# GpSimd's six low parts of weight chunks given to VectorE, and the orders of three engines written anew

## The reference

```
x = x + mla_mixer(rms_norm(x)); x = x + sq_relu_mlp(rms_norm(x))
x = x + moba_mixer(rms_norm(x)); x = x + sq_relu_mlp(rms_norm(x))
h = x + rms_norm_2(gdn_mixer(rms_norm_2(x)))
k, v, c = shared_kv(h)
out = h + rms_norm_2(fox_mixer(rms_norm_2(h), k, v, c))
```

## Time and profile before

| | |
|---|---|
| median of 3 runs | 920.63 us (919.89 to 922.73) |
| the profiled execution's own time | 920.44 us |
| its span, first to last instruction | 918.7 us |
| busy: TensorE, VectorE, ScalarE, GpSimd | 97%, 68%, 57%, 9% |
| mean granted TensorE clock | 0.991 |

### The profile page before, as it was taken

How to read it: one execution, slowest core, us unless ns; L and a number is a source line. 1 busy time by engine, 2 the same in 40 slices (tenths; PEclk the granted TensorE clock), 3 DMA queues, 4 the chain that set the end, 5 groups by cost and what they waited for, 6 DMA issues and landing times.

```text
span 918.7 us, 13095 instructions
## 1 busy us (share of the span) xinstructions
PE 892.3 (97%) x5254; PEld 775.3 (84%) x5254; DVE 623.6 (68%) x1033; ACT 525.6 (57%) x848; POOL 78.4 (9%) x96
## 2 busy tenths in 40 slices
PE   6899999999999999999999999999999999999997
PEld 6877888888888888888888888999988887798885
DVE  6887676766666576657655556696786666776775
ACT  5888544435444686636444434566546565657782
POOL 0055000000000000000000000002536312000000
PEclk9999999999999999999999999999999799999999
DMA  7451456535654544446555654554430041654411
GB/s 261 139 164 67 138 183 247 186 138 184 210 195 145 183 139 146 151 153 238 181 187 182 222 191 138 187 165 157 138 106 32 9 153 46 207 189 180 167 64 46
DMA packets 61677, 142.67 MB, mean 155 GB/s; under 512 B 5296, under 2 KB 7344, under 8 KB 61616
## 3 DMA queue, kind: packets, MB, share of 16 engines
q1 hardware_dynamic: 61616, 141.83, 45.0%
HBM read 140.77 MB, written 1.05 MB: 154 GB/s over the span
## 4 chain that ended last, share of the span: by engine, by line
PE 90%; DVE 3%; POOL 3%; issue 2%; ACT 1%; DMA 1%; SPq 0%; DVEq 0%; ACTq 0%; POOLq 0%
PE ps L491 86%; PE ps L499 4%; POOL arena L3531 3%; DMA X<-x_dram 1%; ACT whi L1382 1%; DVE sub L2315 1%; ACT arena L1382 1%; DVE wlo L2315 0%; DVE xhl L2315 0%; POOL otl L3531 0%; DVE X L2315 0%; DVE arena L2321 0%; DVE arena L2315 0%; ACT otl L1382 0%; DVE X L2321 0%
## 5 line engine op out<-in xcount | busy, mean ns | idle before, releaser
L2315 DVE TENSOR_TENSOR wlo<-raw,whi 128x2048 fp32r<-128x2048 f32 (+3 forms) x130 | 286.8, 2215 | 121.7 <-ACT whi L1382 121.4
L1382 ACT ACTIVATE whi<-raw 128x2048 fp32r<-128x2048 f32 (+3 forms) x136 | 250.7, 1851 | 179.0 <-PE ps L491 164.1
L491 PE MATMUL ps<-xhl,whi 128*128 128x512 f32 (+3 forms) x928 | 216.4, 345 | 0.0
L491 PE MATMUL ps<-whi,xhl 128*128 128x512 f32 (+2 forms) x528 | 168.7, 387 | 1.2 <-DVE xhl L2321 1.0
L491 PE MATMUL ps<-whi,oth 128*128 128x512 f32 x416 | 164.6, 396 | 0.2 <-DVE otl L2321 0.2
L491 PEld LDWEIGHTS ps<-xhl,whi 128*128 128x128 f32 (+2 forms) x928 | 150.8, 187 | 14.4 <-DVE xhl L2321 0.8
L491 PE MATMUL ps<-whi,otl 128*128 128x512 f32 x416 | 162.4, 390 | 0.0
L491 PE MATMUL ps<-wlo,oth 128*128 128x512 f32 x416 | 162.2, 390 | 0.0
L491 PE MATMUL ps<-xhl,wlo 128*128 128x256 f32 x720 | 140.1, 281 | 0.0
L491 PEld LDWEIGHTS ps<-xhl,wlo 128*128 128x128 f32 x720 | 116.8, 187 | 11.2
L491 PEld LDWEIGHTS ps<-whi,xhl 128*128 128x128 f32 x528 | 99.4, 190 | 18.3 <-DVE wlo L2315 1.9
(11 more groups left out here) (146 smaller groups left out, 882.0 us busy)
## 6 DMA issues: line engine op xcount, KB each, us to landing
raw<-mlp_w_in_dram SPq DMA_DIRECT2D x32, 1024.0 KB, 5.4
raw<-mlp_w_out_dram SPq DMA_DIRECT2D x32, 1024.0 KB, 5.0
raw<-gdn_w_in_dram SPq DMA_DIRECT2D x16, 1024.0 KB, 5.3
raw<-moba_w_qkv_dram SPq DMA_DIRECT2D x12, 1024.0 KB, 5.2
raw<-kv_w_dram SPq DMA_DIRECT2D x8, 1024.0 KB, 5.5
raw<-fox_w_in_dram SPq DMA_DIRECT2D x8, 1024.0 KB, 5.3
raw<-mla_w_o_dram SPq DMA_DIRECT2D x4, 1024.0 KB, 5.4
raw<-moba_w_o_dram SPq DMA_DIRECT2D x4, 1024.0 KB, 6.0
```

The costliest lines, as they stand in the source:

```text
L491: return eng.matmul(o, l, r, start=start, stop=True, skip_group_check=True)
L1382: return eng.activation(o, i, f, **kw)
L2315: return eng.tensor_tensor(o, a, b, f)
```

## The change

`ON_POOL` becomes empty, so VectorE makes every low part as a whole chunk, all counted on `s_lod`. GpSimd keeps `q_rope` and the `level` masks; its six `lo` steps are taken out. The wait for the low part of a `uq` chunk moves from quarter 0 to quarter 1. The orders of TensorE, ScalarE and VectorE are written anew in MLA, GDN and at the start of FOX. No step is added or removed but the `lo` ones, SyncE's order stays, and the stages between MLA and GDN keep their orders. The core of the diff, with the indentation of the steps cut: the two single lines, then the orders of TensorE (MLA, GDN), ScalarE (MLA, GDN), VectorE (MLA, GDN) and GpSimd:

```diff
-ON_POOL = {104, 106, 108, 110, 112, 114}
+ON_POOL = set()
 
...
-    if q == 0:
+    if q == (1 if kind == "uq" else 0):
         if kind == "pw" and stage[:3] == "mlp":
...
-to(1, 3)
+to(4, 0)
 bias_mm(0)
-to(4, 0)
 turn_c(0)
 turn_c(1)
 turn_c(2)
 turn_c(3)
-to(4, 1)
 turn_c(4)
-to(5, 2)
+to(6, 2)
 kpe_T()
 to(7, 3)
 k_T(0, 0)
 k_T(0, 1)
-bias_mm(1)
 to(8, 0)
 q_T(0)
+bias_mm(1)
 bias_mm(2)
 qp_T(0)
 q_T(1)
 score_pair(0)
-to(8, 2)
+to(9, 2)
 qp_T(1)
-to(9, 2)
 turn_p("mla", 0)
+turn_p("mla", 1)
 score_pair(1)
-turn_p("mla", 1)
 value("mla", 0)
 value("mla", 1)
-to(10, 2)
+to(10, 3)
 k_T(1, 0)
 k_T(1, 1)
-to(10, 3)
 q_T(2)
 qp_T(2)
 to(11, 0)
...
 score_pair(3)
-to(11, 1)
 turn_p("mla", 4)
+to(11, 3)
 turn_p("mla", 5)
-to(12, 0)
 turn_p("mla", 6)
 value("mla", 4)
 value("mla", 5)
 turn_p("mla", 7)
+to(12, 0)
 value("mla", 6)
 value("mla", 7)
 to(14, 0)
...
-to(97, 1)
+to(97, 3)
 few_T(0)
-to(101, 0)
+to(101, 3)
 cum_mm()
-to(101, 2)
+to(103, 1)
 sums(0)
-to(102, 0)
+to(104, 0)
 sums(1)
-to(103, 0)
+to(105, 0)
 sums(2)
-to(103, 2)
 sums(3)
-to(104, 1)
 sums(4)
-to(104, 3)
 sums(5)
+sums(6)
+sums(7)
 to(105, 3)
-sums(6)
-to(106, 1)
-sums(7)
+rw_T()
+to(106, 0)
+row_bc(0)
+kq(0)
+to(106, 2)
+row_bc(1)
 to(106, 3)
-rw_T()
+row_bc(2)
 to(107, 0)
-row_bc(0)
-row_bc(1)
-kq(0)
-to(107, 1)
-row_bc(2)
+kq(1)
+row_bc(3)
 to(107, 2)
-row_bc(3)
-kq(1)
-to(108, 1)
 kq(2)
+kq(3)
+to(108, 0)
 row_bc(4)
+row_bc(5)
+kq(4)
 to(108, 2)
-kq(3)
-row_bc(5)
-to(109, 0)
-kq(4)
+inv_c(0)
 kq(5)
-to(109, 1)
+to(108, 3)
 row_bc(6)
 row_bc(7)
+to(109, 0)
+inv_r(0)
+to(109, 1)
 kq(6)
 to(109, 2)
 kq(7)
-inv_c(0)
+inv_0(1)
+inv_0(0)
 to(109, 3)
-inv_r(0)
-to(110, 1)
+inv_w(1, 3)
+inv_w(0, 3)
 v_T(0, 0)
-inv_0(0)
-v_T(0, 1)
-inv_0(1)
-inv_w(0, 3)
-v_T(1, 0)
-inv_w(1, 3)
+inv_x(1, 3)
 inv_x(0, 3)
-inv_x(1, 3)
-v_T(1, 1)
+to(110, 0)
 inv_v(0, 3)
 inv_v(1, 3)
 inv_w(1, 4)
+v_T(0, 1)
+v_T(1, 0)
 inv_w(0, 4)
-to(110, 2)
 inv_x(1, 4)
+to(110, 1)
 inv_x(0, 4)
 inv_v(1, 4)
 inv_w(1, 5)
+v_T(1, 1)
 inv_v(0, 4)
 inv_w(0, 5)
 inv_x(1, 5)
+to(110, 2)
 inv_x(0, 5)
 inv_v(1, 5)
 inv_w(1, 6)
 inv_v(0, 5)
 inv_w(0, 6)
-inv_x(1, 6)
 to(110, 3)
 inv_x(0, 6)
+inv_x(1, 6)
 to(111, 0)
 inv_f(0)
 inv_t(0)
...
 inv_y(0)
 inv_t(1)
 inv_r(1)
+sol(1, 0)
 sol(0, 0)
 inv_y(1)
-sol(1, 0)
+sol(0, 1)
 inv_0(3)
 inv_0(2)
+sol(1, 1)
 inv_w(3, 3)
+sol(0, 2)
+sol(2, 0)
+inv_w(2, 3)
+sol(1, 2)
 sol(3, 0)
-inv_w(2, 3)
-sol(2, 0)
 inv_x(3, 3)
-sol(1, 1)
-sol(3, 1)
-sol(0, 1)
 inv_x(2, 3)
...
+hi(2)
 squares("mla")
-hi(2)
 hi(3)
+hi(4)
 rope_sin()
 table("natural_log_exp_and_others")
 rsq("mla_x")
-hi(4)
+proj_scale()
 hi(5)
-hi(6)
-proj_scale()
 c_hi(0)
 c_hi(1)
 c_hi(2)
-c_squares()
 c_hi(3)
 c_hi(4)
+c_squares()
+hi(6)
 rsq("mla_c")
 kv_copy(0, 0)
 kv_copy(0, 1)
...
+kv_copy(1, 0)
 hi(8)
+k_copy(0, 0)
+k_copy(0, 1)
+rsq("mla_q1")
+q_copy(0)
 hi(9)
-k_copy(0, 0)
-rsq("mla_q1")
-k_copy(0, 1)
-kv_copy(1, 0)
-q_copy(0)
 qp_copy(0)
 kv_copy(1, 1)
+k_squares(1)
+q_copy(1)
 hi(10)
-q_copy(1)
-k_squares(1)
 exp("mla", 0)
-qp_copy(1)
 exp("mla", 1)
 divide("mla", 0)
 divide("mla", 1)
+uq_copy(2, 0)
+qp_copy(1)
+uq_copy(2, 1)
+q_squares(2)
+p_copy("mla", 0)
 rsq("mla_k1")
-uq_copy(2, 0)
-uq_copy(2, 1)
-p_copy("mla", 0)
-q_squares(2)
 p_copy("mla", 1)
-uq_copy(3, 0)
+rsq("mla_q2")
 o_hi("mla", 0)
 o_hi("mla", 1)
-rsq("mla_q2")
-exp("mla", 2)
+uq_copy(3, 0)
 uq_copy(3, 1)
 q_squares(3)
-hi(11)
+exp("mla", 2)
 exp("mla", 3)
+divide("mla", 2)
 rsq("mla_q3")
-divide("mla", 2)
 k_copy(1, 0)
 k_copy(1, 1)
 q_copy(2)
+divide("mla", 3)
 qp_copy(2)
-divide("mla", 3)
+hi(11)
 q_copy(3)
 p_copy("mla", 2)
-hi(12)
 p_copy("mla", 3)
+exp("mla", 4)
 qp_copy(3)
-exp("mla", 4)
+divide("mla", 4)
+exp("mla", 5)
 o_hi("mla", 2)
 o_hi("mla", 3)
-exp("mla", 5)
-divide("mla", 4)
+hi(12)
 divide("mla", 5)
 exp("mla", 6)
+exp("mla", 7)
+p_copy("mla", 4)
+divide("mla", 6)
+divide("mla", 7)
+p_copy("mla", 5)
 hi(13)
-exp("mla", 7)
-divide("mla", 6)
-p_copy("mla", 4)
-p_copy("mla", 5)
-divide("mla", 7)
 p_copy("mla", 6)
 o_hi("mla", 4)
 p_copy("mla", 7)
...
+rates()
 hi(100)
-rates()
-conv_acc(2)
-conv_acc(3)
 beta_()
 table("silu_and_others")
+conv_silu(0)
+conv_silu(1)
+conv_acc(2)
 hi(101)
-conv_silu(0)
 hi(102)
-conv_silu(1)
+conv_acc(3)
+conv_acc(4)
 conv_silu(2)
+conv_silu(3)
+hi(103)
 qk_square(0)
-conv_acc(4)
-hi(103)
 conv_acc(5)
-conv_silu(3)
+hi(104)
+conv_acc(6)
 qk_square(1)
-hi(104)
+conv_silu(4)
+hi(105)
+conv_acc(7)
+hi(106)
 qk_square(2)
-qk_square(3)
-conv_acc(6)
-conv_acc(7)
-hi(105)
-conv_silu(4)
 conv_silu(5)
 conv_silu(6)
+conv_silu(7)
+conv_acc(8)
+qk_square(3)
 qk_square(4)
-hi(106)
 qk_square(5)
-conv_silu(7)
 qk_square(6)
-conv_acc(8)
+qk_square(7)
 conv_acc(9)
-qk_square(7)
-hi(107)
 table("natural_log_exp_and_others")
 ln_sums()
+hi(107)
 hi(108)
+decay(0)
+decay(1)
+decay(2)
 conv_acc(10)
 conv_acc(11)
-decay(0)
-decay(1)
+decay(3)
 hi(109)
-decay(2)
-decay(3)
 decay(4)
+decay(5)
 hi(110)
-decay(5)
 decay(6)
 decay(7)
 table("silu_and_others")
-hi(111)
 v_silu(0)
 v_silu(1)
-hi(112)
 inv_0(0)
 inv_0(1)
+inv_w(1, 3)
 inv_w(0, 3)
-inv_w(1, 3)
 inv_y(0, 3)
-z_silu(0, 0)
 inv_y(1, 3)
 inv_w(1, 4)
-z_silu(0, 1)
 inv_w(0, 4)
-z_silu(1, 0)
+hi(111)
 inv_y(1, 4)
 inv_w(1, 5)
 inv_y(0, 4)
 inv_w(0, 5)
+hi(112)
 inv_y(1, 5)
-inv_w(1, 6)
 inv_y(0, 5)
 inv_w(0, 6)
+inv_w(1, 6)
 inv_t(0)
+z_silu(0, 0)
+z_silu(0, 1)
 hi(113)
+sol(1, 0)
+inv_t(1)
+sol(0, 0)
+z_silu(1, 0)
 z_silu(1, 1)
 table("natural_log_exp_and_others")
-inv_t(1)
-sol(1, 0)
-sol(0, 0)
 inv_0(3)
 inv_0(2)
 inv_w(3, 3)
+sol(0, 2)
+sol(2, 0)
+inv_w(2, 3)
 sol(3, 0)
...
-gain("mla")
 xlo("mla", 2)
-xlo("mla", 3)
 lo(1)
 read_positions()
 bias_table()
+xlo("mla", 3)
+lo(2)
+rope_angle()
+mean_x("mla")
+gain("mla")
+lo(3)
 bias_ind(0)
-lo(2)
-mean_x("mla")
-rope_angle()
-lo(3)
+lo(4)
+rsq_b("mla_x")
+rope_cos()
+proj_scale()
 bias_ind(1)
-rope_cos()
-rsq_b("mla_x")
-rope_table()
-proj_scale()
-lo(4)
 c_lo(0)
 c_lo(1)
 c_lo(2)
-bias_add(0)
-lo(5)
+c_lo(3)
+bias_ind(2)
+rope_table()
 c_mean()
-c_lo(3)
 c_lo(4)
 rsq_b("mla_c")
-bias_ind(2)
+lo(5)
+lo(6)
 k_rope()
-lo(6)
 k_sums(0)
 lo(7)
 q_sums(0)
-kp_copy()
 rsq_b("mla_k0")
...
-conv_taps(1)
 rates_in()
 lo(100)
+rates_out()
 conv_pre(2)
+conv_taps(1)
 conv_pre(3)
-rates_out()
+lo(101)
 conv_taps(2)
+conv_pre(4)
 conv_taps(3)
-lo(101)
-conv_pre(4)
 lo(102)
+lo(103)
 conv_pre(5)
 conv_taps(4)
+conv_pre(6)
 conv_taps(5)
-lo(103)
+lo(104)
+conv_pre(7)
+conv_taps(6)
+conv_taps(7)
+lo(105)
+conv_pre(8)
+cum_copy()
+lo(106)
 sum_add(0)
 sum_add(1)
-conv_pre(6)
-conv_pre(7)
-cum_copy()
+conv_pre(9)
 sum_add(2)
-conv_taps(6)
+conv_taps(8)
 sum_add(3)
-conv_taps(7)
-conv_pre(8)
-lo(105)
 sum_add(4)
+conv_taps(9)
 sum_add(5)
-conv_pre(9)
-conv_taps(8)
-conv_taps(9)
 sum_add(6)
-lo(107)
 sum_add(7)
 decay_columns()
 rT_copy()
+lo(107)
+decay_arg(0)
+block_(0)
+lo(108)
+decay_arg(1)
+decay_arg(2)
 conv_pre(10)
 conv_pre(11)
-decay_arg(0)
-decay_arg(1)
-block_(0)
+block_(1)
+decay_arg(3)
 conv_taps(10)
-block_(1)
-decay_arg(2)
-decay_arg(3)
 conv_taps(11)
 block_(2)
+block_(3)
+inv_0(1)
+inv_0(0)
 decay_arg(4)
-inv_0(0)
-block_(3)
 decay_arg(5)
+block_(4)
 lo(109)
-block_(4)
+inv_d(0)
 block_(5)
 decay_arg(6)
 decay_arg(7)
-inv_0(1)
+inv_b(0)
 block_(6)
+inv_e(1)
+inv_e(0)
 block_(7)
-inv_d(0)
-inv_b(0)
-inv_e(0)
-inv_e(1)
 v_beta(0, 0)
+inv_x(1, 3)
+inv_x(0, 3)
+lo(110)
 v_beta(0, 1)
+inv_x(1, 4)
 v_beta(1, 0)
-inv_x(0, 3)
-inv_x(1, 3)
+inv_x(0, 4)
+lo(111)
 v_beta(1, 1)
-lo(111)
-inv_x(1, 4)
-inv_x(0, 4)
 inv_x(1, 5)
 inv_x(0, 5)
+lo(112)
+inv_x(0, 6)
 inv_x(1, 6)
+inv_s(0)
 inv_s(1)
-inv_x(0, 6)
-inv_s(0)
+inv_0(2)
 inv_0(3)
-inv_0(2)
 inv_f(0)
 inv_f(1)
...
+sol(0)
+sol(1)
 inv_x(3, 3)
-sol(1)
+inv_x(2, 3)
+sol(2)
+lo(113)
 sol(3)
-sol(0)
-inv_x(2, 3)
-lo(113)
-sol(2)
 inv_x(2, 4)
 out_sums(0)
 inv_x(3, 4)
 rsq_b("gdn_o0")
 out_norm(0)
 inv_x(2, 5)
+out_sums(1)
 out_lo(0)
-out_sums(1)
 inv_x(3, 5)
 rsq_b("gdn_o1")
 inv_x(2, 6)
+inv_s(2)
 out_norm(1)
-inv_s(2)
 inv_x(3, 6)
+inv_s(3)
 inv_f(2)
-inv_s(3)
 inv_f(3)
 inv_y(2)
 inv_y(3)
 out_lo(1)
+sol(5)
 sol(4)
+sol(6)
 sol(7)
-sol(6)
-sol(5)
 out_sums(2)
 out_sums(3)
 rsq_b("gdn_o2")
 rsq_b("gdn_o3")
 out_norm(2)
 out_norm(3)
+lo(114)
 out_lo(2)
 out_lo(3)
 lo(115)
...
-lo(104)
-lo(106)
-lo(108)
-lo(110)
 level(0, 3)
 level(1, 3)
 level(1, 4)
...
```

More of the change, by code:

```diff
@@ L1271, in tensor_program @@
             inv_w(3, 6)
+            to(111, 1)
+            inv_x(3, 6)
             inv_f(2)
-            inv_x(3, 6)
             inv_t(2)
@@ L1844, in scalar_program @@
             xhi("mlp0", 3)
+            hi(15)
             hi(16)
@@ L2151, in scalar_program @@
             inv_w(3, 3)
+            sol(0, 2)
+            sol(2, 0)
+            inv_w(2, 3)
             sol(3, 0)
-            inv_w(2, 3)
-            sol(2, 0)
             sol(1, 2)
+            sol(1, 3)
             inv_y(3, 3)
             inv_w(3, 4)
-            sol(1, 3)
-            sol(0, 2)
             inv_y(2, 3)
@@ L2162, in scalar_program @@
             sol(0, 3)
+            out_squares(0)
```

(11 more changed lines are left out.)

124 lines of the change are left out of this document (62 added, 62 removed).

## The result

The changed kernel takes 912.34 us (median of 4 runs, 911.17 to 914.14), the kernel before beside it 920.31 us: ratio 0.991, 95% interval 0.9886 to 0.9934. The profiled execution took 914.14 us with a span of 912.4 (before: 918.7), so the two traces account for 6.3 us; the other three runs of the changed kernel had a granted clock of 0.993 to 0.995 where the profiled one had 0.991, and were 1.7 to 3.0 us shorter. What made them shorter no trace shows.

A forecast was written before the change was run, and what follows sets the result against it. The kernel was taken as TensorE's work plus some 11 us of gaps and 5 to 7 of half clock. Gains of 1.8 (MLA) and 0.9 (GDN, FOX) made 2.7 us: 917.9 on the median's scale, range 914 to 923.6.

The forecast's parts named there:

- (b): MLA: TensorE's waits for `q_rope(0)` and `q_rope(1)` go, 1.8 us gained; 0.9 put back for `score_pair(1)` and `qp_copy(1)`.
- (d): MLA: `turn_p(6)` comes earlier while `divide(6)` stands behind `hi(12)`, `exp(6)` and `exp(7)`: 1.2 us lost.
- D: GDN's run of sums: one-column matmuls might bring half clock, 2 to 5.5 us more, 921.5 as the middle; chance 14%.
- The move itself: Six low parts from GpSimd to VectorE, hidden by TensorE: 0 on the path; uncovered, up to 2.3 us for each of three.
- (a): MLA, gap between chunk 3's last matmul and chunk 4's first: 1.2 us gained, between 0 and 2.2.
- (e): GDN, levels of the first inverse: more chunk quarters spread between them against waits of 1.36 us; net 1.0 gained.
- rival C: Inverse's levels in GDN: whole subtractions hold up VectorE's `inv_x` and GpSimd's masks, 924.7 us; chance 13%.
- (f): GDN, `sums(2)` to `sums(7)` in one run of 4.9 us: `qk_square(h)` needs `sums(h-2)`, 0.3 us lost.
- (g): GDN, `rw_T` now ahead of (105, 3): TensorE waits 0 to 1.2 us, 0.6 taken as lost.
- (h): GDN, `inv_f(0)` to `inv_0(3)`: no weight quarter left there, the wait of 1.35 us stays, 0 gained.
- Rival E: Whole kernel: nothing moves, MLA's gain is lost in GDN and to fuller VectorE, 920.6 us; chance 13%.
- rival B: MLA and first levels: all listed waits go, clock stays up for part of 718 to 730, 914 us; chance 18%.

The follow-up runs named there:

- the filled gap: Kernel before with 16 transposes of a constant on TensorE ahead of `turn_c(0)` in MLA: 919.08 us against 921.01, ratio 0.9979.
- the spread sums: Changed kernel with sums of heads 4 and 5 a quarter of chunk 105 later, heads 6 and 7 two quarters later: 910.71 us, ratio 0.9894.
- the two filled kernels: Constant transposes in the idles behind the first inverse: 10 in the kernel before, 917.57 us; 5 and 7 in the changed kernel with sums spread, 909.40 us.

## Why the prediction was wrong

The forecast was 917.9, the range ended at 914.0, and the time is 912.34. The direction was right. The sum failed at two steps: the give-backs charged in MLA, (b) and (d), did not come, and the clock was no term of the sum at all. One rival, D, came true without turning the sum.

- *The move itself, 0.* Right as far as it went: no chunk's first quarter waits for its low part in 602:688. Wrong in what it left out. I had cited the shared interfaces only for GpSimd's masks; what counts is that GpSimd's subtractions stretch VectorE's additions with two SBUF operands by a factor of about four, and its taps. In the old order the taps seldom meet it (the 255-wide ones take 0.511 us there, 0.477 without GpSimd); in the new orders giving the work back costs about 4 us. So 0 was the sum of two large terms that depend on the order.
- *MLA (a), 1.2.* Measured 33.20 - 32.00 = 1.20.
- *MLA (b) to (d), 0.6.* This is the step that failed most: 3.14 were measured. The waits went as said (0.44, 1.33 and 1.53 became 0.23), but the two give-backs, 0.9 at `score_pair(1)` and 1.2 at `turn_p(6)`, did not come: at neither place is there a wait over 0.3 (0.18 at 62.56, 0.26 and 0.20 at 78.53 and 80.12). I had charged a delay of ScalarE's queue in full where weight quarters lay ahead on TensorE. The listed waits shrank by 2.4 us, 0.5 is the clock that no longer falls at chunk 4 (by the filled gap's trace), which I had not put into the sum at all, though the earlier trace rows showed the half speed; 0.2 is spread over waits too short to be listed. By the medians of the filled gap the clock's part is 1.9 us, in which falls elsewhere may have a share.
- *GDN (e), 1.0 of 1.36.* All four waits of the levels went, in spite of three whole subtractions there: rival C is false at its place. The groups of the inverse's small matmuls (687 to 714 us), with equal counts, also lost 0.9 us of busy time, probably waits too short to be listed as idle. With the spread sums the stretch up to `inv_f(0)` is 2.0 us shorter than before, the 0.93 at `rw_T` included.
- *GDN (f), -0.3.* The squares' ring of two costs nothing: TensorE issues the 48 matmuls without a gap. What the run of sums costs is rival D, 2.5 us inside it and 2.2 behind it, 4.7 us of half clock in the profiled run where D said 2 to 5.5. I had given D 14%; its mechanism was right, and its time, 921.5, was not, because the other terms were too small.
- *GDN (g), -0.6.* 0 in the changed kernel, where the half clock makes TensorE late itself; 0.93 when it is not.
- *GDN (h), 0, and the clock behind it.* I wrote that the clock would be low for about 10 us again. In the changed kernel it is low for 3.4 us, from 718.7 (`inv_0(3)` at 719.74 takes 1.97) to 722.1. The waits are hardly smaller than before (0.63 + 1.04 against 1.35 + 0.39). From `inv_f(0)` to FOX the kernel before takes 60.5 us, the changed one 57.0. The trace with the old orders and as short a fall (MLA's gap filled) takes 58.3, so 2.2 us of this are clock, none of which was in the sum, and 1.3 the orders. That clock part is in part luck: the five traces with the old GDN orders and no filling behind the inverse had 10.2, 10.2, 10.2, 6.8 and 3.4 us of half clock there, the seven with the new ones 3.4 four times, 6.8 twice and 10.2 once. Fewer long falls with the new orders are likely, but not shown. What there was of (i) shows between the two filled kernels, 659.81 and 656.98: 2.8 us for all GDN orders and the move together, with the sums spread, where 0.9 was the sum.
- *FOX (k), 0.3.* 0.15.
- *Rival E* is out by every run of the changed kernel; *rival B* (all waits gone, clock up for part of 718 to 730) is the nearest to what happened, with 914, but left out MLA's clock and that the clock's part is a draw.

GDN in one line, MLP to FOX: 663.16 - 3.35 (10.2 us of half clock) - 2.83 (orders and move, sums spread) = 656.98; + 1.17 (3.4 us of half clock behind the inverse) = 658.15; + 3.20 (sums in one run) = 661.35. What stays open: why the fall behind equal waits lasts 3.4 us in one run and 10.2 in another, and where the 1.7 us lie by which the medians gain more than the traces. The runs show that the fall varies (0.95 and 1.00 against 0.91 and 0.92 of clock), not by what.

## What to carry to other kernels

Cost the clock as a term of its own: where TensorE idles about a microsecond amid thin work, look at the matmuls behind the idle, and price both the wait and the half speed. Look inside a run of thin matmuls too: a run that takes too long can be at half speed and not waiting, which the spacing of its matmuls tells. A few transposes of a constant in the gap gave the second back in each of three kernels; the scatter came down where no fall was left (2.9 us in the kernel before, 2.6 and 3.0 with one of its gaps filled, 1.1 with the sums spread, 0.7 with the gaps filled there too). Two single traces whose falls differ in length can't be compared as they stand. A whole-chunk operation moved to another engine costs nothing, or its full length, by what stands right behind it in that queue, so a move and its order are one change. Beside a working GpSimd, count with VectorE's small steps on two SBUF operands being about four times as long, as the additions here were.

## What the runs showed of the hardware

- Idles of 0.63 and 1.04 us with small matmuls between them were enough for a fall to 1.2 GHz, and so was a run of 48 one-column matmuls without a gap: the clock fell 2.5 us after its start (643.6 against 641.08; 2.6 us in the kernel without MLA's orders). The same 48 in groups of 16 with chunk matmuls between them left the clock at full.
- One-column matmuls started 0.112 us apart at full clock and 0.213 at half.
- Behind the first inverse 3.4, 6.8 and 10.2 us of half clock cost 1.16, 2.23 and 3.35 us of the time (660.97, 662.04 and 663.16 against 659.81).
- The fall differs between executions of one program: the kernel without MLA's orders took 915.2 us at a mean clock of 0.995 and 922.0 at 0.986; with the gaps filled, four runs lay within 0.7 us.
- VectorE's additions of 128x32 to 128x48 with both operands in SBUF took 0.76 to 0.86 us beside a working GpSimd and 0.19 to 0.21 without, each ending 0.05 to 0.06 us after an operation of GpSimd; those with one operand in PSUM took 0.19 to 0.21 in both.
